# A hybrid attention and delta-rule layer: w_in products taken in another order around the modulations

## Chip, cores and metric

The kernel runs on one core of a Trainium2 chip. The metric is the device time of one execution in microseconds (us), taken as the median of several runs.

## What is computed

One layer for 256 tokens of width 1024 in float32. The part that matters here is the front: a conditioning vector c gives, through silu and a 1024 x 3072 matrix, a shift, a scale and a gate for every channel; x is normalised and modulated to h; h is multiplied by w_in.

```python
mod = silu(c) @ ada_w + ada_b
shift, scale, gate = split(mod, 3)
h = rmsnorm(x, pre_norm_w) * (1 + scale) + shift
proj = h @ w_in            # 1024 x 4104: q, k, v, gates, delta-rule q, k, v, ...
# behind it: softmax attention (8 heads), short convolution and silu on the
# delta-rule q, k, v, the gated delta rule in chunks of 64, output gates
y = concat(o_moba, o_dn) @ w_out
out = x + gate * rmsnorm(y, post_norm_w)
```

## The kernel before

All products are made in split precision: an operand w is kept as whi (rounded) and wlo (w - whi), h as hhi and hlo, and a product is three matmuls into one PSUM tile: whi with hhi, wlo with hhi, whi with hlo (`three`, L1395, L1396, L1397).

Channels of h are cut into 8 blocks k of 128. Of w_in, the 1536 columns of the delta-rule q, k, v come first: 16 units n of 128 x 768, two for each k (k = n // 2). A unit is 6 tiles of 128 columns, so 18 matmuls of 256 columns (`qkv_products`, `qkv_unit_tile`); the last two units are run together, tile pair by tile pair (`last_qkv_products`), and each finished pair is handed on to the convolution. They start when the split parts of both units 14 and 15 are there. Behind them come the other columns of w_in (`half`), and everything else.

Before a unit n can run:
- its weights must have landed (SyncE issues all loads in a hand-written order), ScalarE must have made whi of it (`hi(n)`, L543), and GpSimd (`lo(n)`, L474) or VectorE (`lo(n)`, L915, for n = 5, 9, 11, 14) must have made wlo; `low_part(n)` names that semaphore;
- its block k of h must be there in both parts.

h comes in pieces p = 0 to 5, of blocks 0, 1, 2, 3, (4, 5) and (6, 7). A piece goes through these steps:
- `mod_sums(p, k0, k1)` on VectorE: a sum over the 8 row blocks of the modulation matrix, weighted with silu(c), first one L932, then six L934, then L936 into `acc`; for pieces 4 and 5 these are 128 x 512;
- `mod(p)` on TensorE (L1458): 4 matmuls with one column (8 for pieces 4 and 5) that turn `acc` into columns of shift and scale;
- `modulate(p)` on VectorE (L945, L947): the columns mod_b and mod_a;
- `modulated(p)` on ScalarE (L582): h of each block into a PSUM bank, then `h_hi(p)` (L593): hhi of each block;
- `h_lo(p)` on VectorE (L906): hlo of each block. It waits for hhi of the whole piece.

Every engine runs its own list in the order in which it is written, and waits on semaphores. The lists around the change, as they are before:
- TensorE: ... unit 3, mod(3), units 4, 5, 6, mod(4), units 7, 8, 9, mod(5), units 10 to 13, the last two.
- ScalarE: ... hi(5), piece 2, piece 3, hi(6), hi(7), hi(8), piece 4, hi(9) to hi(13), piece 5, hi(14), the gates' columns, hi(15), hi(16), first taps of the convolution.
- VectorE: ... rest of sums 3, h_lo(2), lo(5), modulate(3), two sums of piece 4, h_lo(3), six sums of piece 4, two sums of piece 5, modulate(4), two more, h_lo(4), lo(9), the last four sums of piece 5, modulate(5), lo(11), h_lo(5), the gates' low part, lo(14), conv.
- GpSimd: lo(0) to lo(4), lo(6), lo(7), lo(8), lo(10), lo(12), lo(13), lo(15), ...

The wait of a unit stands ahead of all its matmuls:

```python
def qkv_products(n):
    k = n // 2
    pe.wait_ge(hlo_done, k + 1)
    pe.wait_ge(*low_part(n))
    for i in range(6 * (n % 2), 6 * (n % 2) + 6):
        ins = qkv_unit_tile(k, i)
    ins.then_inc(unit_done, 1)
```

Of the kernel before, what the change touches and what calls it, by code (L numbers as in the profile page):

```python
# [32 lines left out]
ACT = mybir.ActivationFunctionType  # L33
# [3 lines left out]
P = 128  # L37
D = 1024
S = 256
# [22 lines left out]
PIECES = [(0, 1), (1, 1), (2, 1), (3, 1), (4, 2), (6, 2)]  # L62
# [10 lines left out]
SPL = 4  # L73
# [8 lines left out]
def build(nc, x, x_turned, ada, gate_w, gate_b, post_w, w_qkv, w_rest, w_gates, w_out, const, out):  # L82
    with ExitStack() as ctx:
        def sb(name, shape, dt=F32, into=ctx):
            return into.enter_context(nc.sbuf_tensor(name, shape, dt))
# [4 lines left out]
        bank = [ctx.enter_context(nc.psum_tensor(f"bank{b}", [P, 512], F32)) for b in range(8)]  # L90
# [12 lines left out]
        mod_a = sb("mod_a", [P, NK])  # L103
        mod_b = sb("mod_b", [P, NK])
# [11 lines left out]
        hhi = sb("hhi", [P, NK, S], F32R)  # L116
        hlo = sb("hlo", [P, NK, S], F32R)
        raw = sb("raw", [P, RAW, UNIT])
        whi = sb("whi", [P, SPL, UNIT], F32R)
        wlo = sb("wlo", [P, SPL, UNIT], F32R)  # L120
# [29 lines left out]
        with ExitStack() as e:  # L150
            xT = sb("xT", [P, NK, S], into=e)
# [14 lines left out]
        with ExitStack() as e:  # L166
# [20 lines left out]
        xsq_done, xsq1_done, xrows_ready, xrows_copied, xsum_ready, xstd_done, xrstd_done, rs_ready, xn_done, expa_done = map(  # L187
            sem, ("xsq_done", "xsq1_done", "xrows_ready", "xrows_copied", "xsum_ready", "xstd_done", "xrstd_done", "rs_ready", "xn_done", "expa_done"))
        acc_done, mod_ready, rows_made, rows_copied, mod_read, h_done, hhi_done, hlo_done = map(
            sem, ("acc_done", "mod_ready", "rows_made", "rows_copied", "mod_read", "h_done", "hhi_done", "hlo_done"))  # L190

        hi_done, lo_done, dve_lo_done, unit_done, group_ready = map(sem, ("hi_done", "lo_done", "dve_lo_done", "unit_done", "group_ready"))
# [34 lines left out]
        def raw_u(n):  # L227
            if n < RAW:
                return raw[:, n, 0:HQ]
            if n < N1:  # L230
                return homes[n - RAW]
            return raw[:, (n - N1) % RAW, :]
# [9 lines left out]
        def split_u(buf, n):  # L242
            return buf[:, n % SPL, 0:(HQ if n < N1 else UNIT)]
# [4 lines left out]
        def two(b):  # L248
            return bank[b][:, :].rearrange("p (a s) -> p a s", a=2)
# [66 lines left out]
        def low_part(n):  # L316

            if n in DVE_LO:
                return dve_lo_done, sum(u <= n for u in DVE_LO)
            return lo_done, n + 1 - sum(u <= n for u in DVE_LO)  # L320
# [209 lines left out]
        def _(act):  # L530
# [7 lines left out]
            def hi(n):  # L538

                act.wait_ge(*loaded(n))  # L540
                if n >= SPL:
                    act.wait_ge(*used_up(n - SPL))
                act.activation(split_u(whi, n), raw_u(n), ACT.Copy).then_inc(hi_done, 1)  # L543
# [31 lines left out]
            def modulated(p):  # L575

                k0, n = PIECES[p]
                act.wait_ge(mod_read, p + 1)
                act.wait_ge(xn_done, p + 1)
                for j in range(n):  # L580
                    k = k0 + j
                    act.activation(two(6 + p % 2)[:, j, :], xT[:, k, :], ACT.Identity, scale=mod_a[:, k:k + 1], bias=mod_b[:, k:k + 1]).then_inc(h_done, 1)  # L582

            def h_hi(p):
                k0, n = PIECES[p]
                if p == 0:
                    act.wait_ge(mod_read, 1)
                    act.wait_ge(xn_done, 1)
                    act.activation(hhi[:, 0, :], xT[:, 0, :], ACT.Identity, scale=mod_a[:, 0:1], bias=mod_b[:, 0:1]).then_inc(hhi_done, 1)
                    return  # L590
                act.wait_ge(h_done, k0 + n)
                for k in range(k0, k0 + n):
                    act.activation(hhi[:, k, :], two(6 + p % 2)[:, k - k0, :], ACT.Copy).then_inc(hhi_done, 1)  # L593

            def ba_hi():
                act.wait_ge(wba_loaded, 16)
                act.activation(wbs[:, :, 0:8], wba[:, :, :], ACT.Copy).then_inc(wba_hi, 1)
# [163 lines left out]
            hi(6)  # L761
            hi(7)
            hi(8)
            modulated(4)
            h_hi(4)
            hi(9)
            hi(10)
            hi(11)
            hi(12)
            hi(13)  # L770
            modulated(5)
            h_hi(5)
            hi(14)
            ba_hi()
            hi(15)
            hi(16)
# [83 lines left out]
        def _(dve):  # L860
# [51 lines left out]
            def lo(n):  # L912

                dve.wait_ge(hi_done, n + 1)
                dve.tensor_tensor(split_u(wlo, n), raw_u(n), split_u(whi, n).bitcast(F32), ALU.subtract).then_inc(dve_lo_done, 1)  # L915
# [5 lines left out]
            def mod_sums(p, k0, k1):  # L921

                n = 256 * PIECES[p][1]
                a = bank[6 + p % 2][:, 0:n]
                if k0 == 0:
                    dve.wait_ge(hlo_done, PIECES[p - 1][0])
                for k in range(k0, k1):
                    w, c_k = ada_piece(p)[:, k, :], sml[:, 24 + k:25 + k]
                    if k % 2 == 0:
                        dve.wait_ge(*ada_ready(p, k))  # L930
                    if k == 0:
                        link(dve.tensor_scalar(a, w, c_k, None, ALU.mult))  # L932
                    elif k < NK - 1:
                        link(dve.scalar_tensor_tensor(a, w, c_k, a, ALU.mult, ALU.add))  # L934
                    else:
                        dve.scalar_tensor_tensor(acc[:, p % 2, 0:n], w, c_k, a, ALU.mult, ALU.add).then_inc(acc_done, 1)  # L936

            def modulate(p):

                k0, n = PIECES[p]  # L940
                k2, b = slice(k0, k0 + n), bank[mod_bank(p)]
                dve.wait_ge(mod_ready, p + 1)
                if p == 0:
                    dve.wait_ge(scale_done, 1)
                dve.tensor_tensor(mod_b[:, k2], b[:, 0:n], pcol[:, R_SHIFT + k0:R_SHIFT + k0 + n], ALU.add)  # L945
                for k in range(k0, k0 + n):
                    ins = dve.scalar_tensor_tensor(mod_a[:, k:k + 1], b[:, n + k - k0:n + k - k0 + 1], scale1[:, k:k + 1],  # L947
                                                   pcol[:, R_PRE + k:R_PRE + k + 1], ALU.add, ALU.mult)
                ins.then_inc(mod_read, 1)
# [303 lines left out]
            mod_sums(3, 4, 8)  # L1253
            h_lo(2)
            lo(5)
            modulate(3)
            mod_sums(4, 0, 2)
            h_lo(3)
            mod_sums(4, 2, 4)
            mod_sums(4, 4, 8)  # L1260
            mod_sums(5, 0, 2)
            modulate(4)
            mod_sums(5, 2, 4)
            h_lo(4)
            lo(9)
            mod_sums(5, 4, 8)
            modulate(5)
            lo(11)
            h_lo(5)
# [122 lines left out]
        def _(pe):  # L1392
# [58 lines left out]
            def mod(p):  # L1451

                if p < ROWS:
                    pe.wait_ge(rows_copied, p + 1)
                else:
                    pe.wait_ge(acc_done, p - ROWS + 1)
                for i in range(2 * PIECES[p][1]):
                    ins = pe.matmul(bank[mod_bank(p)][:, i:i + 1], acc[:, p % 2, i * P:(i + 1) * P], epsc[:, 2:3] if p < ROWS else ones[:, 0:1],  # L1458
                                    start=True, stop=True)
                ins.then_inc(mod_ready, 1)  # L1460

            def qkv_unit_tile(k, i):
                n, o = 2 * k + i // 6, (i % 6) * P
                return three(bank[i // 2][:, (i % 2) * S:(i % 2 + 1) * S], w_parts, h_parts,
                             (slice(None), n % SPL, slice(o, o + P)), (slice(None), k, slice(None)),
                             start=(k == 0 and i % 2 == 0), stop=(k == NK - 1), skip=True)
# [6 lines that stand above are left out]
                for i in range(6 * (n % 2), 6 * (n % 2) + 6):  # L1473
                    if k == 0 and i == 10:
                        pe.wait_ge(xn_done, len(PIECES))
                    ins = qkv_unit_tile(k, i)
                ins.then_inc(unit_done, 1)

# [354 lines left out]
            mod(2)  # L1833
            qkv_products(2)
            qkv_products(3)
            mod(3)
            qkv_products(4)
            qkv_products(5)
            qkv_products(6)
            mod(4)  # L1840
            qkv_products(7)
            qkv_products(8)
            qkv_products(9)
            mod(5)
            qkv_products(10)
            qkv_products(11)
            qkv_products(12)
            qkv_products(13)
            last_qkv_products()
            ba()  # L1850
# [168 lines left out]
```

## Time and profile before

| | |
|---|---|
| median of 3 runs | 190.93 us (190.72 to 196.72) |
| the profiled execution, its own time | 190.73 us |
| span of that execution, first to last instruction | 188.9 us |
| around the span (190.73 - 188.9) | 1.8 us |
| TensorE busy | 178.0 us (94%) |
| VectorE busy | 141.5 us (75%) |
| ScalarE busy | 101.5 us (54%) |
| GpSimd busy | 77.5 us (41%) |
| mean granted TensorE clock | 0.996 |
| the 16 units, first to last matmul start | 14.14 to 56.58 us |

How to read it: times are counted from the start of the span. The ends of matmuls are modelled, so a matmul of 256 columns is shown with 0.28 us though the next begins 0.12 us later; it is the starts that tell. An L number is a line of the kernel. Idle time of an engine matters only where the engine is the bound of that stretch.

### The profile page before, as it was taken

Reading aid. Unit: us, or ns where it says so; the run is one execution under the profiler, and the core shown is the slowest. Engines: PE = TensorE matmul, PEld = TensorE weight load, DVE = VectorE, ACT = ScalarE, POOL = GpSimd, SP = SyncE. Lnnn points to the kernel's source line nnn. Section 1 sums busy time; section 2 is a strip of 40 time slices with the busy share of each in tenths; the row PEclk is TensorE's granted clock in tenths of the full one; section 3 lists DMA queues with packets and bytes.
Section 4 is the critical chain, followed back from the end, with each engine's and each line's share of the span. In section 5 each row is a group of like instructions: output and inputs, shape, how many; then the busy total and the mean of one; then the engine's idle time right before and its main releaser. Section 6 shows DMA issues by size and latency. Waiting matters only on the chain.

```text
span 188.9 us, 4380 instructions
## 1 busy us (share of the span) xinstructions
PE 178.0 (94%) x1718; PEld 161.5 (85%) x1718; DVE 141.5 (75%) x345; ACT 101.5 (54%) x195; POOL 77.5 (41%) x42
## 2 busy tenths in 40 slices
PE   7999989889999998999999999999999999999980
PEld 6769879789999998998998999999998987888850
DVE  0359699893459988998999787889689777858074
ACT  2645444439368878956562270455384448636230
POOL 2036627335687922985055068224913200810000
PEclk9999999999999999999999999999999999999998
DMA  5999999999519980300901807006942983020023
GB/s 160 403 386 394 393 409 407 407 397 404 218 16 367 395 328 8 114 0 2 323 14 17 319 8 212 13 0 220 362 201 78 344 356 119 14 97 0 3 111 111
DMA packets 12246, 38.41 MB, mean 203 GB/s; under 512 B 1473, under 2 KB 1857, under 8 KB 11714
## 3 DMA queue, kind: packets, MB, share of 16 engines
q1 hardware_dynamic: 12082, 37.61, 53.6%
q10 hardware_dynamic: 144, 0.52, 0.8%
q8 instruction: 14, 0.23, 0.5%
q14 instruction: 6, 0.05, 0.1%
HBM read 37.08 MB, written 1.05 MB: 202 GB/s over the span
## 4 chain that ended last, share of the span: by engine, by line
PE 69%; DVE 16%; DMA 6%; SPq 5%; issue 2%; ACT 1%; POOL 1%; DVEq 0%; POOLq 0%; ACTq 0%
PE bank L1395 16%; PE bank L1397 15%; PE bank L1396 15%; DVE cv L958 6%; DMA ada<-in_ada 6%; DVE bank L934 4%; SPq L351 3%; PE bank L1641 3%; PE bank L1630 3%; PE bank L1738 2%; PE bank L1745 2%; SPq L368 1%; PE bank L1754 1%; PE bank L1604 1%; PE bank L1666 1%
## 5 line engine op out<-in xcount | busy, mean ns | idle before, releaser
L474 POOL TENSOR_TENSOR wlo<-raw,whi 128x1024 fp32r<-128x1024 f32 (+1 forms) x25 | 58.1, 2334 | 62.2 <-ACT whi L543 62.2
L1395 PE MATMUL bank<-hhi,whi 128*128 128x256 f32 x218 | 63.1, 289 | 1.6 <-DVE hlo L906 1.1
L1396 PE MATMUL bank<-hhi,wlo 128*128 128x256 f32 x218 | 61.6, 283 | 0.0
L1397 PE MATMUL bank<-hlo,whi 128*128 128x256 f32 x218 | 61.6, 283 | 0.0
L1395 PEld LDWEIGHTS bank<-hhi,whi 128*128 128x128 f32 x218 | 41.7, 191 | 3.3 <-issue 1.8
L543 ACT ACTIVATE whi<-raw 128x1024 fp32r<-128x1024 f32 (+1 forms) x33 | 33.3, 1023 | 16.5 <-PE bank L1397 7.4
L1396 PEld LDWEIGHTS bank<-hhi,wlo 128*128 128x128 f32 x218 | 41.8, 192 | 0.0
L1397 PEld LDWEIGHTS bank<-hlo,whi 128*128 128x128 f32 x218 | 41.7, 191 | 0.0
L958 DVE SCALAR_TENSOR_TENSOR cv<-bank,convh,cv 128x255 f32<-128x255 f32 (+2 forms) x36 | 17.0, 481 | 5.6 <-ACT cv L609 4.6
L934 DVE SCALAR_TENSOR_TENSOR bank<-ada,sml,bank 128x256 f32<-128x256 f32 (+1 forms) x24 | 14.9, 621 | 0.7
L1157 DVE SCALAR_TENSOR_TENSOR accg<-ada,sml,accg 128x512 f32<-128x512 f32 x16 | 12.0, 751 | 2.7 <-DMA ada<-in_gate_w 2.3
L1395 PE MATMUL bank<-whi,ohi 128*128 128x512 f32 x32 | 12.6, 393 | 0.0
L1397 PE MATMUL bank<-wlo,ohi 128*128 128x512 f32 x32 | 12.5, 390 | 0.0
L672 ACT ACTIVATE pr<-bank,stat 128x128 f32<-128x128 f32 (+1 forms) x16 | 6.5, 420 | 11.1 <-DVE stat L1122 11.1
L1396 PE MATMUL bank<-whi,olo 128*128 128x512 f32 x32 | 12.4, 389 | 0.0
L915 DVE TENSOR_TENSOR wlo<-raw,whi 128x1024 fp32r<-128x1024 f32 x8 | 9.8, 1222 | 0.8 <-ACT whi L543 0.6
L488 POOL TENSOR_TENSOR rot<-rot,cst 128x512 f32<-128x512 f32 x4 | 4.4, 1092 | 12.5 <-DVE rot L1097 11.8
L1395 PE MATMUL bank<-whi,hhi 128*128 128x256 f32 x32 | 9.2, 286 | 0.0
L1396 PE MATMUL bank<-whi,hlo 128*128 128x256 f32 x32 | 9.1, 283 | 0.0
L1397 PE MATMUL bank<-wlo,hhi 128*128 128x256 f32 x32 | 9.0, 283 | 0.0
L1406 PE MATMUL bank<-ones 128*128 128x256 f32 x22 | 7.9, 530 | 1.1 <-DVE ones L868 1.1
L1406 PEld LDWEIGHTS bank<-ones 128*128 128x128 f32 x22 | 5.9, 279 | 2.3 <-DVE ones L868 1.0
(223 smaller groups left out, 337.6 us busy)
## 6 DMA issues: line engine op xcount, KB each, us to landing
raw<-in_w_rest SPq DMA_DIRECT2D x20, 512.0 KB, 4.8
ada<-in_ada SPq DMA_DIRECT2D x16, 256.0 KB, 7.1
ada<-in_ada SPq DMA_DIRECT2D x8, 512.0 KB, 12.0
ada<-in_gate_w SPq DMA_DIRECT2D x4, 1024.0 KB, 6.9
raw<-in_w_out SPq DMA_DIRECT2D x8, 512.0 KB, 5.7
raw<-in_w_qkv SPq DMA_DIRECT2D x5, 384.0 KB, 8.2
qkvs<-in_w_qkv SPq DMA_DIRECT2D x4, 384.0 KB, 11.2
cv<-in_w_qkv SPq DMA_DIRECT2D x4, 384.0 KB, 12.7
```

The lines of the kernel that those rows point to most:

```text
L351: sp.dma_start(ada_piece(p)[:, 2 * g:2 * g + 2, :].rearrange("p k n -> p (k n)"), ada[:, o:o + n * 512]).then_inc(ada_ready(p, 2 * g)[0], 16)
L474: pool.tensor_tensor(split_u(wlo, n), raw_u(n), split_u(whi, n).bitcast(F32), ALU.subtract).then_inc(lo_done, 1)
L543: act.activation(split_u(whi, n), raw_u(n), ACT.Copy).then_inc(hi_done, 1)
L672: act.activation(pr[:, e, o:o + w], bank[ATT[e]][:, o:o + w], ACT.Exp, scale=AD ** -0.5, bias=stat[:, 16 + i:17 + i], accum_out=stat[:, 32 ...
L915: dve.tensor_tensor(split_u(wlo, n), raw_u(n), split_u(whi, n).bitcast(F32), ALU.subtract).then_inc(dve_lo_done, 1)
L934: link(dve.scalar_tensor_tensor(a, w, c_k, a, ALU.mult, ALU.add))
L958: ins = dve.scalar_tensor_tensor(cv[:, i, j:], b[:, 0:S - j], w, cv[:, i, j:], ALU.mult, ALU.add)
L1157: dve.scalar_tensor_tensor(a, adag[:, k, :], sml[:, 24 + k:25 + k], a, ALU.mult, ALU.add).then_inc(gate_acc, 1)
L1395: pe.matmul(out, a[0][ia], b[0][ib], start=start, stop=False, skip_group_check=skip)
L1396: pe.matmul(out, a[1][ia], b[0][ib], start=False, stop=False, skip_group_check=skip)
L1397: return pe.matmul(out, a[0][ia], b[1][ib], start=False, stop=stop, skip_group_check=skip)
L1406: pe.matmul(bank[b][:, 0:256], ones[:, :], ones[:, 0:1].to_broadcast([P, 256]), start=True, stop=True)
```

## The change

On TensorE, units 4, 6, 8 and 12 take the six tiles' products with hhi first (12 matmuls) and the six with hlo last, and wait for hlo only ahead of those (`qkv_h_lo_last`). Units 9, 10 and 11 take the products with whi first and those with wlo last, and wait for wlo only there (`qkv_w_lo_last`). mod(3) stands behind unit 4 instead of ahead of it, mod(4) amid unit 7 after four of its six tiles (`qkv_around_mod`) instead of ahead of it, mod(5) behind unit 10 instead of ahead of it. On ScalarE pieces 4 and 5 go block by block (`h_two`). On VectorE two sums of piece 4 stand ahead of modulate(3) instead of behind it, and one sum of piece 5 is moved from ahead of modulate(4) to behind it. The number of matmuls is the same.

```diff
+            def h_two(p):
+                k0, n = PIECES[p]
+                act.wait_ge(mod_read, p + 1)
+                act.wait_ge(xn_done, p + 1)
+                for k in range(k0, k0 + n):
+                    act.activation(two(6 + p % 2)[:, k - k0, :], xT[:, k, :], ACT.Identity, scale=mod_a[:, k:k + 1], bias=mod_b[:, k:k + 1]).then_inc(h_done, 1)
+                    act.wait_ge(h_done, k + 1)
+                    act.activation(hhi[:, k, :], two(6 + p % 2)[:, k - k0, :], ACT.Copy).then_inc(hhi_done, 1)
...
-            modulated(4)
-            h_hi(4)
+            h_two(4)
...
-            modulated(5)
-            h_hi(5)
+            h_two(5)
...
+            mod_sums(4, 0, 2)
             modulate(3)
-            mod_sums(4, 0, 2)
+            mod_sums(4, 2, 3)
             h_lo(3)
-            mod_sums(4, 2, 4)
-            mod_sums(4, 4, 8)
-            mod_sums(5, 0, 2)
+            mod_sums(4, 3, 8)
+            mod_sums(5, 0, 1)
             modulate(4)
-            mod_sums(5, 2, 4)
+            mod_sums(5, 1, 3)
             h_lo(4)
             lo(9)
-            mod_sums(5, 4, 8)
+            mod_sums(5, 3, 8)
             modulate(5)
...
+            def qkv_first_parts(n, second, n0=0, n1=6):
+
+                k = n // 2
+                for i in range(6 * (n % 2) + n0, 6 * (n % 2) + n1):
+                    o = (i % 6) * P
+                    out = bank[i // 2][:, (i % 2) * S:(i % 2 + 1) * S]
+                    w, h = whi[:, n % SPL, o:o + P], hhi[:, k, :]
+                    pe.matmul(out, w, h, start=False, stop=False, skip_group_check=True)
+                    if second == "w_lo":
+                        pe.matmul(out, wlo[:, n % SPL, o:o + P], h, start=False, stop=False, skip_group_check=True)
+                    else:
+                        pe.matmul(out, w, hlo[:, k, :], start=False, stop=False, skip_group_check=True)
+
+            def qkv_h_lo_last(n):
+
+                k = n // 2
+                pe.wait_ge(hhi_done, k + 1)
+                pe.wait_ge(*low_part(n))
+                qkv_first_parts(n, "w_lo")
+                pe.wait_ge(hlo_done, k + 1)
...
+            def qkv_w_lo_last(n):
+
+                k = n // 2
+                pe.wait_ge(hlo_done, k + 1)
+                pe.wait_ge(hi_done, n + 1)
+                qkv_first_parts(n, "h_lo")
+                pe.wait_ge(*low_part(n))
...
+            def qkv_around_mod(n, p):
+
+                k = n // 2
+                pe.wait_ge(hlo_done, k + 1)
+                pe.wait_ge(*low_part(n))
+                for i in range(6 * (n % 2), 6 * (n % 2) + 6):
+                    if i % 6 == 4:
+                        mod(p)
+                    ins = qkv_unit_tile(k, i)
+                ins.then_inc(unit_done, 1)
...
+            qkv_h_lo_last(4)
             mod(3)
-            qkv_products(4)
             qkv_products(5)
-            qkv_products(6)
-            mod(4)
-            qkv_products(7)
-            qkv_products(8)
-            qkv_products(9)
+            qkv_h_lo_last(6)
+            qkv_around_mod(7, 4)
+            qkv_h_lo_last(8)
+            qkv_w_lo_last(9)
+            qkv_w_lo_last(10)
             mod(5)
-            qkv_products(10)
-            qkv_products(11)
-            qkv_products(12)
+            qkv_w_lo_last(11)
+            qkv_h_lo_last(12)
             qkv_products(13)
             last_qkv_products()
```

## Rows read from the trace of the kernel before

**Rows 1.** The page's first part: busy time of each engine.

```profile
PE 178.0 (94%) x1718; PEld 161.5 (85%) x1718; DVE 141.5 (75%) x345; ACT 101.5 (54%) x195; POOL 77.5 (41%) x42
```

**Rows 2.** Who waited for whom, 15 to 70 us: us in total, times, longest.

```profile
PE bank L1458 <- DVE acc L936: 1.7, 3, 0.8
...
PE bank L1395 <- DVE hlo L906: 1.1, 1, 1.1
...
PEld bank L1395 <- issue: 0.8, 2, 0.4
```

**Rows 3.** Timeline of TensorE, 17 to 53 us: start, us, what, idle before.

```profile
17.27 0.35 PE L1395 MATMUL bank<-hhi,whi 128*128 128x256 f32 x1 [0.38 <-POOL wlo L474]
...
26.15 0.61 PE L1458 MATMUL bank<-ones,acc 128*128 128x1 f32 x4 [0.83 <-DVE acc L936]
26.61 0.36 PE L1395 MATMUL bank<-hhi,whi 128*128 128x256 f32 x1
...
31.31 0.36 PE L1395 MATMUL bank<-hhi,whi 128*128 128x256 f32 x1
...
34.06 1.05 PE L1458 MATMUL bank<-ones,acc 128*128 128x1 f32 x8 [0.36 <-DVE acc L936]
...
38.44 0.39 PE L1395 MATMUL bank<-hhi,whi 128*128 128x256 f32 x1 [1.06 <-DVE hlo L906]
...
42.85 0.95 PE L1458 MATMUL bank<-ones,acc 128*128 128x1 f32 x8
43.66 0.36 PE L1395 MATMUL bank<-hhi,whi 128*128 128x256 f32 x1
...
52.38 0.28 PE L1395 MATMUL bank<-hhi,whi 128*128 128x256 f32 x1
```

**Rows 4.** Timeline of VectorE, 27 to 45 us.

```profile
27.21 0.15 DVE L945 TENSOR_TENSOR mod_b<-bank,cst 128x1 f32<-128x1 f32 x1
27.28 0.21 DVE L947 SCALAR_TENSOR_TENSOR mod_a<-bank,scale,cst 128x1 f32<-128x1 f32 x1
27.40 0.75 DVE L932 TENSOR_SCALAR bank<-ada,sml 128x512 f32<-128x512 f32 x1
...
29.31 3.91 DVE L934 SCALAR_TENSOR_TENSOR bank<-ada,sml,bank 128x512 f32<-128x512 f32 x5
...
37.96 0.76 DVE L906 TENSOR_TENSOR hlo<-bank,hhi 128x256 fp32r<-128x256 f32 x2 [0.43 <-ACT hhi L593]
...
43.84 0.16 DVE L945 TENSOR_TENSOR mod_b<-bank,cst 128x2 f32<-128x2 f32 x1 [1.23 <-PE bank L1458]
...
44.16 0.95 DVE L915 TENSOR_TENSOR wlo<-rot,whi 128x768 fp32r<-128x768 f32 x1
```

**Rows 5.** Timeline of ScalarE, 24 to 50 us.

```profile
24.77 0.38 ACT L593 ACTIVATE hhi<-bank 128x256 fp32r<-128x256 f32 x1
27.52 0.57 ACT L582 ACTIVATE bank<-xT,mod_b,mod_a 128x256 f32<-128x256 f32 x1 [2.37 <-DVE mod_a L947]
28.12 0.39 ACT L593 ACTIVATE hhi<-bank 128x256 fp32r<-128x256 f32 x1
28.40 0.84 ACT L543 ACTIVATE whi<-early 128x768 fp32r<-128x768 f32 x1
...
48.77 0.84 ACT L543 ACTIVATE whi<-cv 128x768 fp32r<-128x768 f32 x1 [1.12 <-DMA cv<-in_w_qkv]
```

**Rows 6.** Timeline of GpSimd, 15 to 50 us.

```profile
15.29 1.83 POOL L474 TENSOR_TENSOR wlo<-raw,whi 128x768 fp32r<-128x768 f32 x1 [1.64 <-ACT whi L543]
...
29.31 1.85 POOL L474 TENSOR_TENSOR wlo<-early,whi 128x768 fp32r<-128x768 f32 x1 [4.72 <-ACT whi L543]
...
49.69 1.84 POOL L474 TENSOR_TENSOR wlo<-cv,whi 128x768 fp32r<-128x768 f32 x1 [1.06 <-ACT whi L543]
```

**Rows 7.** Stretches: busy us of PE, PEld, DVE, ACT, POOL, then TensorE's granted clock.

```profile
37.20:38.50 1.30, 0.23 (x3) 0.06 (x1) 0.87 (x3) 1.30 (x4) 0.00 (x0) 1.00 1.01 392
...
187.00:188.00 1.00, 0.00 (x0) 0.00 (x0) 0.00 (x0) 0.00 (x0) 0.00 (x0) 0.72 0.93 342
```

More of the change, by code:

```diff
@@ L1475, in qkv_products @@
                         pe.wait_ge(xn_done, len(PIECES))
+                    ins = qkv_unit_tile(k, i)
[18 more added lines that the diff above has]
+                for i in range(6 * (n % 2), 6 * (n % 2) + 6):
+                    o = (i % 6) * P
+                    ins = pe.matmul(bank[i // 2][:, (i % 2) * S:(i % 2 + 1) * S], whi[:, n % SPL, o:o + P], hlo[:, k, :],
+                                    start=False, stop=False, skip_group_check=True)
+                ins.then_inc(unit_done, 1)
+            def qkv_w_lo_last(n):
[4 more added lines that the diff above has]
+                pe.wait_ge(*low_part(n))
+                for i in range(6 * (n % 2), 6 * (n % 2) + 6):
+                    o = (i % 6) * P
+                    ins = pe.matmul(bank[i // 2][:, (i % 2) * S:(i % 2 + 1) * S], wlo[:, n % SPL, o:o + P], hhi[:, k, :],
+                                    start=False, stop=False, skip_group_check=True)
+                ins.then_inc(unit_done, 1)
+            def qkv_around_mod(n, p):
+                k = n // 2
+                pe.wait_ge(hlo_done, k + 1)
+                pe.wait_ge(*low_part(n))
+                for i in range(6 * (n % 2), 6 * (n % 2) + 6):
+                    if i % 6 == 4:
+                        mod(p)
                     ins = qkv_unit_tile(k, i)
```

## The prediction

> **What bounds the kernel now.** I read the busy shares first: TensorE is at work for 94% of the span [rows 1], so what counts is when it stands still, and the change touches only the stretch of the 16 units. Then who waited for whom there [rows 2]: TensorE waited 1.7 us for sums of VectorE ahead of mod(), 1.1 us for hlo, and its weight load is shown with 0.8 us of "issue", a wait with no releaser named. Third, TensorE's timeline [rows 3], which turns this into places. A unit without a stop takes 18 x 0.12 = 2.16 us, and the first matmul behind a stop costs 0.08 us more: units 10 to 13 run from 43.66 to 52.38, 8.72 us = 4 x 2.16 + 0.08. mod() with 4 matmuls takes 0.46 us (26.15 to 26.61), with 8 it takes 0.81 us (42.85 to 43.66). The stops, counted from the slot that was free (0.16 us ahead of a modelled end):
> - ahead of mod(3): 25.16 to 26.15, 0.99 us;
> - ahead of unit 6: 26.61 + 0.08 + 2 x 2.16 = 31.01, start 31.31, 0.30 us;
> - ahead of mod(4): 31.31 + 0.08 + 2.16 = 33.55, start 34.06, 0.51 us;
> - ahead of unit 8: 34.06 + 0.81 + 0.08 + 2.16 = 37.11, start 38.44, 1.33 us by this count.
>
> Together 3.1 us, and mod(5) and all behind it up to 52.38 run without a stop. The last pair of units starts at 52.38; VectorE's convolution and the rest of TensorE's list hang on that start, so I take it as the time that the change moves.
>
> **Behind the stops: the chain of the weights.** Unit 6 is the one to look at, since the waits view names nobody for it. GpSimd's lo(6) runs 29.31 + 1.85 = 31.16 [rows 6] and unit 6 starts at 31.31, 0.15 us later. At unit 1, where the profile does name GpSimd, lo(1) ends at 15.29 + 1.83 = 17.12 and the matmul starts at 17.27: the same 0.15 us [rows 3, 6]. So lo(6) released unit 6. lo(6) began 0.07 us behind hi(6) on ScalarE (28.40 + 0.84 = 29.24), and hi(6) came directly behind the two steps of piece 3 (27.52, 28.12), which began 0.03 us after VectorE's modulate(3) was done (27.28 + 0.21 = 27.49) [rows 4, 5]. So modulate(3) holds not only piece 3 of h but also unit 6's weights: from its end to the start of unit 6 it is 31.31 - 27.49 = 3.82 us.
>
> **The change part by part, in TensorE's new order.**
>
> Unit 4 ahead of mod(3). It needs hhi of block 2, done at 24.77 + 0.38 = 25.15 [rows 5], so it starts at about 25.2, runs 12 matmuls to 26.7, and hlo of block 2 is made by 26.5 (0.42 us directly behind the sum that released mod(3) at 26.15): no second stop. It ends at 25.2 + 0.08 + 2.16 = 27.44. The 0.99 us are gone. mod(3) costs 0.46: 27.90.
>
> modulate(3) later. Two sums of 512 columns now stand ahead of it on VectorE. A sum takes 3.91 / 5 = 0.78 us, 0.79 with its step [rows 4]. They begin at 27.21 where modulate(3) began, if the data have landed (they had by 27.40, [rows 4], so at most 0.19 us is open), and mod_a is done at 27.49 + 2 x 0.79 = 29.07 instead of 27.49. mod(3) itself, done near 28.05, doesn't hold it. ScalarE then does piece 3 from 29.10, hhi(3) at 30.09, and hi(6) from 29.98 to 30.82.
>
> Unit 6. lo(6) on GpSimd: 30.89 to 32.74. Unit 5 ends at 27.90 + 0.08 + 2.16 = 30.14. Unit 6 takes its hhi products first, but those include wlo with hhi, so its first wait is for lo(6) too: start 32.74 + 0.15 = 32.89. A stop of 2.75 us where there were 0.30, and unit 6 is 1.58 us later than before (32.89 against 31.31), exactly the two sums. Everything won at mod(3) waits here. hlo(3) is made at about 30.5, long before its turn: that late wait is worth nothing in this unit.
>
> Unit 7 around mod(4). Unit 6 ends at 32.89 + 2.24 = 35.13; lo(7) follows lo(6), 32.74 + 1.85 = 34.59, in time. Sums 4: one from 28.99, then h_lo(3) near 30.1 to 30.47, then five, 30.47 + 5 x 0.79 = 34.4. mod(4) comes after four tiles, 35.13 + 1.44 = 36.57, so its 0.51 us stop is gone. It is read by VectorE 0.99 us after its start, as mod(5) was (42.85 to 43.84), at 37.56; ScalarE is released 0.44 us later, 38.0. The two tiles left run 36.57 + 0.81 + 0.08 + 0.72 = 38.18.
>
> Unit 8. With h_two the first hhi is there 0.99 us after ScalarE's start (27.52 to 28.12 + 0.39, [rows 5]), 38.99; unit 8 starts at 39.1, a stop of 0.9 us in place of 1.33, 0.65 us later than before. The second block follows 0.9 us later (the next instruction begins 0.28 us behind L593), so hhi(5) is at 39.9 and h_lo(4), which waits for both, makes hlo(4) by 40.4 (0.42 us each in the pair, [rows 4]); the six hlo products are due at 39.1 + 0.08 + 1.44 = 40.6. No stop. Without h_two and the late wait the start would be at about 40.5: these two edits are worth 1.4 us here.
>
> Units 9 and 10. hi(9) 39.8 to 40.6, lo(9) on VectorE 40.7 to 41.6, due at 42.8; hi(10) to 41.4, lo(10) on GpSimd to 43.3, due at 44.9. Both covered by the late wait for wlo. 41.34 + 2 x 2.16 = 45.66.
>
> mod(5). The last five sums of piece 5 begin behind lo(9): 41.53 + 5 x 0.79 = 45.5, just ahead of 45.66, no stop. mod(5) to 46.47. modulate(5) starts at 46.65, lo(11) 0.32 us behind it [rows 4] ends at 46.97 + 0.95 = 47.92; unit 11 wants it at 46.47 + 0.08 + 1.44 = 47.99. Covered by 0.07 us; if it misses, the price is the miss plus 0.15.
>
> Units 11 to 13. h_two(5) starts at 47.1, hhi(6) 48.1 ahead of unit 12 at 48.71; hlo(6) at 49.45, due 50.15. Last start: 46.47 + 0.08 + 3 x 2.16 = 53.03. hi(14), the gates' columns and hi(15) on ScalarE end near 50.8, lo(14) on VectorE near 51.8 and lo(15) on GpSimd at 52.65: in time, 0.4 us of cover.
>
> The sum: 53.03 - 52.38 = +0.65 us. Check by stops: taken away 0.99 + 0.30 + 0.51 + 1.33 = 3.13; put in 0.04 (unit 4) + 2.75 + 0.92 = 3.71, difference 0.58, the rest is rounding in the modelled mod(4). Regrouped matmuls cost nothing: the same 18 loads and 18 products in a unit, each step still 0.12 us; no row shows a wait inside a unit that is already met; bounds by the nearest row, the 0.08 us of a restart, are one lost or one won at each of the seven new waits, so -0.56 to +0.56, and I take 0, since the waits at unit starts that are already met show none. SyncE's queue isn't moved: the sums of piece 3, for which load of piece 5 waits, end as before. Behind 53.03 the convolution and all after it shift with the start. Against the profiled execution: 190.73 + 0.65 = 191.4; the median lies 0.2 above it, so I forecast 191.5.
>
> **Rivals.**
> (a) Unit 6 isn't held by GpSimd, as the view's "issue" would have it [rows 2]. Then units 4 to 6 run from 25.2 to 32.4, mod(4) waits for the sums (34.4) inside unit 7, and the last start would be near 50.95. But another limit stands there: hi(15) waited for its DMA until 48.77 [rows 5], lo(15) ran 49.69 + 1.84 = 51.53 [rows 6], plus 0.15 = 51.68. So the gain ends at 52.38 - 51.68 = 0.70 us, 190.2. For it: the name in the view. Against it: the 0.15 us that fits twice, and lo(6)'s place in the list. The same time is the floor for any way in which the stops vanish.
> (b) The clock falls in the new stop ahead of unit 6, the longest in this stretch. The granted clock stayed at 1.00 (2.4 GHz) over the present stop at 37.2 to 38.5; it is 0.72 in 187 to 188, falling towards 1.2 GHz, 4 us after TensorE's last matmul [rows 7]. A stop of 2.75 us lies between. If it falls, unit 6 runs at half speed from 32.89: 18 x 0.12 = 2.16 us more (an estimate from the full-speed step), and with mod(4), units 7 and 8 behind it, the end is 0.65 + 2.16 = 2.8 us late, 193.7; two units of it, 195.9. It decides from the point where the stop is long enough for the gate. The Trainium skill ("TensorE: Matmul & The Clock Gate", "Why this matters for your kernels") warns of just this: an idle gap between bursts of matmuls can send the clock back to half. By that rule this change is slower than its ledger; the trace has a fall only behind a longer silence, so it gets a small chance.
> (c) The thin covers (lo(11) 0.07, mod(5) 0.15, lo(15) 0.4 us) fail together: at most some 0.8 us more, 192.3.
>
> **How the numbers follow.** Forecast 0.65, rival (a) 0.22, (b) 0.06, (c) 0.07. The range of 189.8 to 192.6 holds the forecast with the 0.56 us of the new waits either way, (a) with 0.4 us to spare, and (c); (b) is left out. Faster by over 2% means below 187.1, slower means above 194.7; 2% is about what a measurement of this kernel tells from no change. Only the two-unit form of (b) reaches beyond on the slow side, and on the fast side rival (a)'s floor speaks against it: 0.02 faster, 0.95 within, 0.03 slower.
>
> **What would show it.** Right: in the new trace L945 of piece 3 starts near 28.8, hi(6) near 30.0, lo(6) near 30.9, and unit 6 stands until 32.9; no stop ahead of mod(3), mod(4), mod(5); a stop of 0.9 us ahead of unit 8; the last pair of units starting near 53.0 instead of 52.38. Wrong: unit 6 starts by 31 while lo(6) still runs (then (a)), the granted clock is under 1.00 behind 32.9 (then (b)), or the last pair starts where I say and the end doesn't follow, because something behind the convolution waits for its data.

## The result, and the profile after

The changed kernel takes 193.19 us (median; 193.04 to 193.75 in four runs) against 191.36 us, or 190.93 us without an execution of 196.72; the ratio without that one is 1.0119, with a 95% interval of 1.0099 to 1.0138. It is 2.3 us slower, where 0.65 us slower was forecast, and outside the range of 189.8 to 192.6. The profiled execution took 193.75 us with a span of 191.8 us and a mean granted clock of 0.988 (before: 190.73, 188.9 and 0.996). Some executions of every kernel, that of 196.72 among them, take 4 to 8 us longer at a lower mean clock; no ratio or time below counts them, and where such a one was profiled (the filled stop, and before with the sums ahead) its clock is 1.00 up to 145 us, behind every row shown from it.

First TensorE's timeline of the kernel after, around units 4 to 8 (start, us, what, idle before; L1465 is mod(), L1493 and L1495 the products with hhi of the regrouped units, L1508 their products with hlo, L1402 to L1404 the old form):

```profile
25.49 0.38 PE L1493 MATMUL bank<-hhi,whi 128*128 128x256 f32 x1
...
27.74 0.50 PE L1465 MATMUL bank<-ones,acc 128*128 128x1 f32 x4
28.10 0.36 PE L1402 MATMUL bank<-hhi,whi 128*128 128x256 f32 x1
...
33.14 0.36 PE L1493 MATMUL bank<-hhi,whi 128*128 128x256 f32 x1 [2.65 <-POOL wlo L474]
...
34.30 0.41 PE L1495 MATMUL bank<-hhi,wlo 128*128 128x256 f32 x1
34.51 0.41 PE L1493 MATMUL bank<-hhi,whi 128*128 128x256 f32 x1
34.73 0.41 PE L1495 MATMUL bank<-hhi,wlo 128*128 128x256 f32 x1
...
36.65 0.41 PE L1402 MATMUL bank<-hhi,whi 128*128 128x256 f32 x1
...
38.29 0.95 PE L1465 MATMUL bank<-ones,acc 128*128 128x1 f32 x8
...
40.83 0.39 PE L1493 MATMUL bank<-hhi,whi 128*128 128x256 f32 x1 [0.77 <-ACT hhi L602]
```

The stops ahead of mod(3) and mod(4) [rows 3] are gone. In their place stands one of 2.65 us ahead of unit 6 (2.80 from slot to slot), and now the profile names GpSimd as its releaser. From 33.7 us on the matmuls behind it start 0.21 us apart instead of 0.12. The stretches of the same profile say why (busy PE, PEld, DVE, ACT, POOL, then the granted clock):

```profile
32.00:33.00 1.00, 0.00 (x0) 0.00 (x0) 0.96 (x2) 0.00 (x0) 1.00 (x2) 1.00 1.02 390
33.00:34.00 1.00, 0.86 (x6) 0.89 (x7) 0.93 (x3) 0.85 (x1) 1.00 (x1) 0.86 1.01 400
34.00:35.00 1.00, 1.00 (x7) 1.00 (x6) 1.00 (x2) 0.00 (x0) 1.00 (x2) 0.50 1.02 399
...
36.00:37.00 1.00, 1.00 (x6) 1.00 (x6) 0.00 (x0) 0.00 (x0) 0.57 (x1) 0.50 1.06 414
37.00:38.00 1.00, 1.00 (x10) 1.00 (x9) 0.00 (x0) 0.00 (x0) 0.00 (x0) 0.93 0.96 380
```

The granted clock goes to 1.2 GHz (0.50) at about 33.7 us, half a microsecond after unit 6 started and not while TensorE stood, and is back at 2.4 GHz at 37.1. Unit 6 takes 36.65 - 33.14 = 3.51 us instead of 2.24, and the four tiles of unit 7 take 1.64 instead of 1.44: 1.47 us in all.

The chain that makes the stop, on VectorE (first fence), ScalarE (second) and GpSimd (third) of the kernel after:

```profile
27.50 0.75 DVE L939 TENSOR_SCALAR bank<-ada,sml 128x512 f32<-128x512 f32 x1
28.28 0.76 DVE L941 SCALAR_TENSOR_TENSOR bank<-ada,sml,bank 128x512 f32<-128x512 f32 x1
29.07 0.16 DVE L952 TENSOR_TENSOR mod_b<-bank,cst 128x1 f32<-128x1 f32 x1
```

```profile
29.40 0.57 ACT L582 ACTIVATE bank<-xT,mod_b,mod_a 128x256 f32<-128x256 f32 x1 [3.96 <-DVE mod_a L954]
30.00 0.39 ACT L593 ACTIVATE hhi<-bank 128x256 fp32r<-128x256 f32 x1
30.28 0.84 ACT L543 ACTIVATE whi<-early 128x768 fp32r<-128x768 f32 x1
```

```profile
31.19 1.81 POOL L474 TENSOR_TENSOR wlo<-early,whi 128x768 fp32r<-128x768 f32 x1 [6.30 <-ACT whi L543]
...
45.06 3.64 POOL L474 TENSOR_TENSOR wlo<-cv,whi 128x768 fp32r<-128x768 f32 x2
```

Against [rows 4 to 6]: modulate(3) starts at 29.07 instead of 27.21, hi(6) at 30.28 instead of 28.40, lo(6) at 31.19 instead of 29.31: 1.9 us each, of which 0.29 us is an offset that this trace has before any of the edits can act (the first sum of piece 3 starts at 22.04 instead of 21.75). The forecast had 28.8, 30.0 and 30.9 without that offset. The last pair of units starts at 54.86 instead of 52.38, and the convolution 2.48 us later (56.65 against 54.17). The span grew by 2.9 us: some 0.4 us more came behind that start, and no run tells from what.

### The profile page after: what moved, and what is told of

Same layout as the page of the kernel before. It is cut to its first block, busy times and chain, and to the rows that moved or that the text cites. A ratio compares the mean times of both kernels' runs of the same rounds, so it can differ in the third digit from the quotient of the medians.

```text
span 191.8 us, 4383 instructions
## 1 busy us (share of the span) xinstructions
PE 179.8 (94%) x1718; PEld 163.1 (85%) x1718; DVE 140.6 (73%) x345; ACT 101.6 (53%) x195; POOL 77.4 (40%) x42
## 3 DMA queue, kind: packets, MB, share of 16 engines
HBM read 37.08 MB, written 1.05 MB: 199 GB/s over the span
## 4 chain that ended last, share of the span: by engine, by line
PE 69%; DVE 13%; DMA 5%; SPq 5%; issue 2%; ACT 2%; POOL 2%; DVEq 0%; ACTq 0%; POOLq 0%
PE bank L1402 13%; PE bank L1403 13%; PE bank L1404 13%; DVE cv L965 6%; DMA ada<-in_ada 5%; SPq L351 3%; PE bank L1698 3%; PE bank L1687 3%; PE bank L1493 3%; DVE bank L941 2%; PE bank L1795 2%; PE bank L1802 2%; PE bank L1508 1%; SPq L368 1%; PE bank L1495 1%
## 5 line engine op out<-in xcount | busy, mean ns | idle before, releaser
L1402 PE MATMUL bank<-hhi,whi 128*128 128x256 f32 x176 | 51.1, 290 | 0.4 <-POOL wlo L474 0.4
L1403 PE MATMUL bank<-hhi,wlo 128*128 128x256 f32 x176 | 49.9, 283 | 0.0
L1404 PE MATMUL bank<-hlo,whi 128*128 128x256 f32 x176 | 49.7, 283 | 0.0
L1402 PEld LDWEIGHTS bank<-hhi,whi 128*128 128x128 f32 x176 | 33.8, 192 | 1.8 <-issue 1.7
L1403 PEld LDWEIGHTS bank<-hhi,wlo 128*128 128x128 f32 x176 | 33.8, 192 | 0.0
L1404 PEld LDWEIGHTS bank<-hlo,whi 128*128 128x128 f32 x176 | 33.8, 192 | 0.0
L1493 PE MATMUL bank<-hhi,whi 128*128 128x256 f32 x42 | 11.3, 303 | 3.4 <-POOL wlo L474 2.6
L1402 PE MATMUL bank<-whi,ohi 128*128 128x512 f32 x32 | 12.6, 392 | 0.0
L1404 PE MATMUL bank<-wlo,ohi 128*128 128x512 f32 x32 | 12.5, 390 | 0.0
L1493 PEld LDWEIGHTS bank<-hhi,whi 128*128 128x128 f32 x42 | 8.4, 200 | 3.9 <-issue 2.8
L1402 PE MATMUL bank<-whi,hhi 128*128 128x256 f32 x32 | 9.2, 286 | 0.0
L1404 PE MATMUL bank<-wlo,hhi 128*128 128x256 f32 x32 | 9.0, 283 | 0.0
```

The costliest lines, as they stand in the source:

```text
L1402: pe.matmul(out, a[0][ia], b[0][ib], start=start, stop=False, skip_group_check=skip)
L1403: pe.matmul(out, a[1][ia], b[0][ib], start=False, stop=False, skip_group_check=skip)
L1404: return pe.matmul(out, a[0][ia], b[1][ib], start=False, stop=stop, skip_group_check=skip)
L1493: pe.matmul(out, w, h, start=False, stop=False, skip_group_check=True)
```

## The experiments

Each ratio is against the kernel before, run on the same chip in turns; its runs took 190.6 to 191.9 us. "Over before" is the ratio turned into us. "Clock" is the mean granted clock of a run; the kernel before had 0.991 to 0.999 in its runs.

**Filling the stop.** TensorE gets something to do ahead of unit 6 that is short enough not to hold unit 6 up: 20 matmuls whose weights, the tile `zero`, are all 0, so that the sums stay as they are. The lines that make `zero` are left out here.

```diff
+            def fill(n):
+                pe.wait_ge(zero_set, 1)
+                for _ in range(n):
+                    pe.matmul(bank[0][:, 0:S], zero[:, :], hhi[:, 0, :], start=False, stop=False, skip_group_check=True)
...
             qkv_products(5)
+            fill(20)
             qkv_h_lo_last(6)
```

> The kernel after, with TensorE's stop ahead of unit 6 filled by 20 matmuls with an all-zero stationary tile, added to the sums (they add 0; 20 x 0.12 = 2.4 us, less than the 2.9 us from slot to slot of the stop, so unit 6 still starts when lo(6) releases it). Theory (the stop itself costs 0.6 us over before, and the clock that falls behind it costs the other 1.5 us): granted clock 1.00 from 30 to 40 us, unit 6 starts at the same time as after (about 33.1), the last pair of units 1.5 us earlier than after; time 0.7 us over before, about 191.9. Rival (the clock is no part of it, the regrouped matmuls or the waits between them cost the 2 us): the time stays that of after, 2 us over before. Rival (the clock falls whatever TensorE does there): clock 0.5 near 34 us as after, and 2 us over before.

Measured: ratio 1.0084 (1.0059 to 1.0110), so 1.6 us over before, and a clock of 0.993 to 0.998. TensorE's timeline of this kernel:

```profile
30.05 2.56 PE L1546 MATMUL bank<-hhi,zero 128*128 128x256 f32 x20
32.87 0.36 PE L1499 MATMUL bank<-hhi,whi 128*128 128x256 f32 x1 [0.27 <-POOL wlo L478]
...
36.54 0.95 PE L1471 MATMUL bank<-ones,acc 128*128 128x1 f32 x8
...
48.97 0.98 PE L1527 MATMUL bank<-hhi,wlo 128*128 128x256 f32 x6 [0.84 <-DVE wlo L928]
```

The clock stays at 1.00, and from unit 6 to mod(4) it is 36.54 - 32.87 = 3.67 us, where the kernel after needs 38.29 - 33.14 = 5.15: the 1.5 us are back at this place. So it is behind the empty stop that the clock falls, and with the stop filled it didn't, by the mean clock of all nine counted executions of the two filled kernels (0.993 to 0.998); and the regrouped matmuls cost nothing (unit 4 of the kernel after takes 27.74 - 25.49 = 2.25 us, where 2.24 were reckoned). But the total got only some 0.7 us of it, and by the totals alone even that is not clear of noise (the kernel after had 1.0099 to 1.0138): a new stop of 0.84 us stands amid unit 11, where the kernel after has none. VectorE and GpSimd of the filled kernel there, then VectorE of the kernel after:

```profile
46.97 1.95 DVE L928 TENSOR_TENSOR wlo<-rot,whi 128x768 fp32r<-128x768 f32 x1
```

```profile
44.46 3.64 POOL L478 TENSOR_TENSOR wlo<-cv,whi 128x768 fp32r<-128x768 f32 x2 [1.12 <-ACT whi L547]
```

```profile
48.73 0.95 DVE L922 TENSOR_TENSOR wlo<-rot,whi 128x768 fp32r<-128x768 f32 x1
```

lo(11) on VectorE takes 1.95 us instead of 0.95 [rows 4]. It ends at 48.92, 0.82 us behind the end of GpSimd's lo(12) and lo(13) at 48.10, as if it had stood until GpSimd was done; two runs below test that. In the kernel after lo(11) began at 48.73, GpSimd's pair ended at 45.06 + 3.64 = 48.70, and it took 0.95 us. The fall of the clock had moved it out of the way, by 0.03 us.

**The sums behind modulate(3) again.** The rest is the kernel after.

```diff
-            mod_sums(4, 0, 2)
             modulate(3)
-            mod_sums(4, 2, 3)
+            mod_sums(4, 0, 2)
             h_lo(3)
+            mod_sums(4, 2, 3)
```

> The kernel after, with the two sums of piece 4 put back behind modulate(3) on VectorE. Theory: modulate(3) is then released by mod(3) at about 28.3 instead of 29.1, hi(6) and lo(6) come 0.8 us earlier, the stop ahead of unit 6 is about 2.0 us in place of 2.9, the granted clock stays at 1.00; the time is that of before within 0.4 us. Rival (clock no part): only the 0.8 us come back, 1.4 us over before. Rival (2.0 us of standing still already drops the clock): 1.3 us over before, with a clock of 0.5 behind unit 6's start.

Measured: ratio 1.0037 (0.9998 to 1.0077), but the mean hides two kinds of run. Seven took 191.0 to 191.7 us at a mean clock of 0.991 to 0.998, three took 193.0 to 193.5 at 0.987 or 0.988. The profiled one is of the second kind:

```profile
32.24 0.36 PE L1493 MATMUL bank<-hhi,whi 128*128 128x256 f32 x1 [1.85 <-POOL wlo L474]
```

```profile
33.00:34.00 1.00, 1.00 (x7) 1.00 (x6) 0.96 (x2) 0.75 (x1) 1.00 (x2) 0.52 1.02 401
```

The stop is 0.80 us shorter, as expected, and yet the clock fell in this execution (0.52, where a mean of 1.00 was expected): by time and mean clock the theory and its second rival are both right, in different executions of one kernel, though only the kind with the fall was profiled. A fall costs this kernel 2.0 us (193.2 against 191.2, means of the two kinds), not the 1.3 of the rival. Some 0.3 us of it stand amid unit 11 in the profile, where lo(11), begun at 47.83 beside GpSimd's lo(13), takes 1.40 us. Without a fall, and with the two sums back in their place, the change costs no time that can be told from noise.

**hi(6) ahead of piece 3 on ScalarE.**

```diff
+            hi(6)
             modulated(3)
             h_hi(3)
-            hi(6)
```

> The kernel after, with hi(6) ahead of piece 3 on ScalarE, where ScalarE waits 4 us. Theory: lo(6) is done before 30.3, unit 6 starts as soon as unit 5 and hhi of block 3 are there (about 30.5), no clock fall; a short stop (0.3 to 0.5 us) for lo(7) ahead of unit 7; the gain is then capped by lo(15), whose weights come by DMA, at 0.7 us under before, so 0.3 to 0.8 us faster than before. Rival (something else than the weights holds unit 6): the stop stays, 2 us over before.

Measured: ratio 0.9994 (0.9963 to 1.0025). Eight of nine runs took 190.7 to 191.3 us, 0.2 us under before; one took 193.19 at a mean clock of 0.983, and why isn't known. The stop ahead of unit 6 is gone (it starts at 30.22), the one ahead of unit 7 is 0.34 us, as expected; but most of the gain isn't there. It is spent in the same place as in the filled kernel (TensorE, then VectorE):

```profile
32.97 0.36 PE L1402 MATMUL bank<-hhi,whi 128*128 128x256 f32 x1 [0.34 <-POOL wlo L474]
...
47.23 0.98 PE L1521 MATMUL bank<-hhi,wlo 128*128 128x256 f32 x6 [0.96 <-DVE wlo L922]
```

```profile
45.10 2.07 DVE L922 TENSOR_TENSOR wlo<-rot,whi 128x768 fp32r<-128x768 f32 x1
```

**The kernel before with the sums ahead of modulate(3), nothing else.**

```diff
-            modulate(3)
             mod_sums(4, 0, 2)
+            modulate(3)
```

> The kernel before, with one edit alone: the two sums of piece 4 ahead of modulate(3). TensorE's order is that of before, with mod(3) ahead of unit 4. Theory: hi(6) and lo(6) 1.58 us later, unit 6 starts at 32.9, a stop of 1.9 us in place of 0.3; the stop ahead of mod(4) is 0.1 to 0.5 us, unit 8 is about 1.15 us late, the clock stays at 1.00 because the stop is 1.9 us and not 2.9; 1.1 us over before. Rival (a stop of 1.9 us drops the clock too): 2.5 us over before, granted clock 0.5 near 34 us. Rival (the sums are not what delays unit 6): same time as before.

Measured: ratio 1.0086 (1.0056 to 1.0115), 1.6 us over before, at a clock of 0.992 to 0.994. The two sums alone, in TensorE's old order, make the kernel slower, with no fall of the clock:

```profile
32.92 0.36 PE L1395 MATMUL bank<-hhi,whi 128*128 128x256 f32 x1 [1.68 <-POOL wlo L474]
...
39.49 0.39 PE L1395 MATMUL bank<-hhi,whi 128*128 128x256 f32 x1 [0.91 <-DVE hlo L906]
...
47.72 0.36 PE L1395 MATMUL bank<-hhi,whi 128*128 128x256 f32 x1 [0.60 <-DVE wlo L915]
```

Unit 6 starts at 32.9, as expected, and unit 8 1.05 us late, where 1.15 was. The 0.5 us beyond the forecast are the third row: unit 11 waits for lo(11), which took 2.34 us here, from 45.23 on, beside GpSimd's lo(12).

**lo(11) ahead of modulate(5), with hi(6) first.** This tests the meeting of the two engines; it is the kernel of the hi(6) run with one more edit.

```diff
+            lo(11)
             modulate(5)
-            lo(11)
```

> The kernel after with hi(6) ahead of piece 3 (as in the run with that edit alone, which measured no difference from before), and lo(11) on VectorE ahead of modulate(5) instead of behind it. Theory (VectorE's subtraction lo(11) cannot run while GpSimd's lo(12) or lo(13) runs, which cost 0.96 us ahead of unit 11's last products): lo(11) runs at about 43.7, as soon as hi(11) is done and before lo(12) begins, in 0.95 us; the stop of 0.96 us amid unit 11 is gone; the last pair of units is then held by lo(15), near 51.7; 0.7 us faster than before. Rival (the stop amid unit 11 came from the load of its weights): hi(11) stays at 42.9, so the stop stays, same time as before.

Measured: ratio 0.9968 (0.9956 to 0.9981), 190.14 to 190.89 in six runs, 0.6 us faster than before, where 0.7 was expected. VectorE, and the only stop of TensorE between the start of unit 8 and the end of the units:

```profile
44.03 0.96 DVE L922 TENSOR_TENSOR wlo<-rot,whi 128x768 fp32r<-128x768 f32 x1 [0.31 <-ACT whi L543]
```

```profile
51.97 0.36 PE L1402 MATMUL bank<-hhi,whi 128*128 128x256 f32 x1 [0.53 <-POOL wlo L474]
```

lo(11) takes 0.96 us. It is not quite done (44.99) when GpSimd's lo(12) begins at 44.80, but it came first, and the price falls on GpSimd: its pair takes 3.71 us instead of 3.64. The stop amid unit 11 is gone. What holds the last pair of units now is lo(15), the cap of rival (a). This version beats both kernels, the one before by 0.3%.

**lo(11) ahead of modulate(5), in the filled kernel.** The same edit there.

> The kernel with the filled stop, and lo(11) ahead of modulate(5). Theory: the 0.84 us stop amid unit 11, which the filled kernel has and the kernel after does not, comes from the meeting of lo(11) with GpSimd's lo(13); ahead of modulate(5) lo(11) meets lo(12) only and is done by 47.2, before unit 11 wants it; 0.8 us less than the filled kernel, so 0.8 us over before, which is what the stop ahead of unit 6 alone costs. Rival (the filled kernel is slow for another reason): 1.6 us over before, as the filled kernel.

Measured: ratio 1.0036 (1.0019 to 1.0052), 0.7 us over before. lo(11) met lo(12) alone (45.34 to 47.12), and the 0.84 us are back. What is left is close to what the ledger of the prediction gave for the stop without a fall of the clock, 0.65 us; the last pair of units starts at 53.20, 0.2 us of it waiting for lo(15), which the prediction had given 0.4 us of cover.

**The same edit in the kernel after.**

> The kernel after with lo(11) ahead of modulate(5), no other edit. In the kernel after lo(11) begins 0.03 us behind the end of GpSimd's lo(13) and takes 0.95 us. Theory: moved ahead it starts at 47.1 amid lo(12) and lo(13), takes until one of them ends, at the latest 49.5, and modulate(5) and piece 5 of h are up to 1.1 us late; unit 12 waits for hhi; 0.3 to 0.6 us slower than after, 2.6 us over before. Rival (the two engines do not hold each other up): lo(11) 0.95 us, same time as after.

Measured: ratio 1.0123 (1.0077 to 1.0169). The mean again covers two kinds. Two executions took 193.94 and 194.33 us at a mean clock of 0.990 and 0.986, 2.9 us over before, where the kernel after is 2.3 over: that is the way I expected (2.6), but on two executions. The third, 192.09 us at 0.998, is the profiled one, and the most telling of the study, because in it the clock did not fall:

```profile
33.35 0.36 PE L1493 MATMUL bank<-hhi,whi 128*128 128x256 f32 x1 [2.63 <-POOL wlo L474]
```

```profile
34.00:35.00 1.00, 1.00 (x11) 1.00 (x10) 0.96 (x3) 0.09 (x1) 1.00 (x2) 1.00 1.03 401
```

A stop of 2.63 us with a clock of 1.00 behind it, and a time 0.9 us over before. My expectation for lo(11) had taken the fallen clock's timetable for granted: without the fall it met lo(12) alone and lasted 1.80 us, within its cover.

**The load of unit 15 earlier**, on top of the best version.

```diff
             load_unit(14)
+            load_unit(15)
             load_unit(19)
             load_unit(17)
             load_gates()
             load_unit(18)
-            load_unit(15)
```

> The same as the kernel with hi(6) and lo(11) first, and the load of unit 15 issued directly behind that of unit 14 instead of behind those of four others. Theory (the DMA of unit 15 and lo(15) cap the gain): hi(15) no longer waits for a DMA, the last pair of units starts near 51.4, 0.9 to 1.0 us faster than before. Rival (another limit right behind it, such as lo(14) or unit 16's weights for the first half): 0.7 us faster, as without the new load order.

Measured: ratio 0.9997 (0.9972 to 1.0023). Of twelve runs five took 190.0 to 190.4 us at 0.993 to 0.996, the other seven 191.0 to 192.1 at 0.987 to 0.992. In the profiled one (190.13) hi(15) no longer waits and the stop at the last pair is gone, but TensorE then waits longer ahead of the gates' matmuls, 1.44 us instead of 0.82. A second set of runs was to show where the clock falls in the slower executions (its text counts six and six where the runs are five and seven):

> The kernel with unit 15's load early, unchanged: of its 12 runs 6 took 190.0 to 190.4 us at a mean clock of 0.993 to 0.996, and 6 took 191.0 to 192.1 us at 0.987 to 0.992. Theory: the slower ones hold a clock fall of about 3 us at half speed, in or behind the 1.4 us stop near 71 us ahead of the gates' matmuls, which is longer than in before (0.8 us). Rival: it lies at the stops of the units (30 to 40 us). The profile shows the place if its run is one of the slower kind.

Measured: ratio 1.0004 (0.9976 to 1.0032), again two kinds (190.3 to 190.95 at 0.993 to 0.997, 191.3 to 191.9 at 0.986 to 0.989). The profiled one was of the first kind, with a stop of 1.86 us at 71.51 and a clock of 1.00 on both sides of it. Where the clock falls in the others is open. On the mean the early load of unit 15 gains nothing over the best version (1.0004 and 0.9997 against 0.9968): its quicker kind, 190.2 us in the first set, is 0.3 us under the best version's mean of 190.5, and its slower kind takes the gain away.

**The kernel after again.**

> The kernel after, unchanged, to see how its time goes with the granted clock of each run. Theory (the clock falls behind the stop of 2.8 us ahead of unit 6 in most runs, not in all; where it doesn't, lo(11) meets GpSimd's lo(13) as in the filled kernel and costs 0.84 us): runs with a mean clock over 0.991 take 1.5 to 1.7 us more than before, runs under 0.989 take 2.1 to 2.4 us more; most are of the second kind. Rival (the fall costs its whole 1.5 us): runs over 0.991 take 0.6 to 0.8 us more than before.

Measured: ratio 1.0122 (1.0096 to 1.0148). Four runs at 0.989 or 0.990 took 193.02 to 193.95, 2.3 us over the 191.2 of before; one at 0.993 took 192.90, 1.7 over. The profiled one shows 0.50 from 34 to 37 us. It fits the theory, but the kind without a fall is one run.

**Piece 4 and unit 8 as before**, on the best version.

```diff
-            h_two(4)
+            modulated(4)
+            h_hi(4)
...
-            qkv_h_lo_last(8)
+            qkv_products(8)
```

> The kernel with hi(6) and lo(11) first, with piece 4 of h and unit 8 as in the kernel before (both blocks modulated, then both hhi, and unit 8 waiting for hlo ahead of its first matmul). Theory (the split is worth about 1.4 us at unit 8, of which 0.5 us was spent standing ahead of the last pair of units anyway): the stop ahead of unit 8 is 2.3 us instead of 0.9, the 0.5 us stop ahead of the last pair is gone, 0.9 us slower than the kernel with both edits, 0.2 us over before; a clock fall in some runs is possible. Rival (the late wait is worth nothing): same time as the kernel with both edits.

Measured: ratio 1.0103 (1.0070 to 1.0136), 2.5 us slower than with the split instead of 0.9. The longer stop is as expected, the total isn't:

```profile
38.45 0.39 PE L1403 MATMUL bank<-hhi,whi 128*128 128x256 f32 x1 [2.06 <-DVE hlo L914]
```

```profile
40.00:54.00 14.00, 14.00 (x108) 14.00 (x106) 6.50 (x13) 6.90 (x11) 7.46 (x5) 0.88 0.72 283
```

The stop ahead of unit 8 is 2.06 us instead of 0.77, 1.3 us longer (the prediction gave the split 1.4 us), and behind it the clock falls: a mean of 0.88 over 14 us is 3.4 us at half speed (0.12 x 14 / 0.5). All four runs were at 0.981 to 0.990.

## Why the prediction was wrong

The step that failed is rival (b): the fall of the clock behind the new stop got a chance of 0.06, no term in the sum and no room in the range. It came in nearly every execution and took 1.47 us at units 6 and 7. With the forecast's 0.65 us for the stop that makes 2.1 of the 2.3 us measured. A second step failed unseen beneath it, the cover of lo(11). The rest of the ledger held.

- Unit 4 ahead of mod(3), the sums ahead of modulate(3), hi(6), lo(6), the stop ahead of unit 6: all came as worked out, within 0.1 us once the 0.29 us offset of this trace is taken off (unit 6: 32.89 forecast, 33.14 - 0.29 = 32.85). That lo(6) released unit 6, read from a match of 0.15 us, was right; rival (a) is out.
- mod(4) without a stop, 0.9 us ahead of unit 8, units 9, 10 and 11 covered by the late wait, lo(11) covered by 0.07 us: all as forecast, the last of them by luck, as told below. With the 1.47 us of the clock and the offset added, unit 8 was due at 40.86 (it started at 40.83) and the last pair at 54.79 (54.86).
- Where the clock stays up and lo(11) is out of the way (the filled kernel with lo(11) first), the time is 0.7 us over before, beside the forecast of 0.65. The one profiled execution of the unfilled stop without a fall (lo(11) first) is 0.9 us over.
- The clock. I set a stop of 2.75 us between one of 1.3 us without a fall and a silence of 4 us with one, and gave the fall 0.06. It came in both profiles of the kernel after, by the mean clock in eight of its nine runs, and in two of three of the kernel with lo(11) first, which has the same stop. The Trainium skill ("TensorE: Matmul & The Clock Gate", "Why this matters for your kernels") advises against idle gaps between bursts of matmuls, though its figure is for gaps somewhat longer than this one. The traces go further than the page: the clock fell behind 2.65 and 2.64 us in the kernel after and behind 1.85 us in the run with the sums behind modulate(3). And the profiled execution of the kernel with lo(11) first (2.63 us, clock 1.00) shows that such a gap need not do it. The price of a fall, too, was taken from a wrong step: a matmul is 0.21 us apart at 1.2 GHz, not 0.24, so 1.5 us and not 2.2.
- A term was missing, and the fall hid it. The fall costs 1.5 us where it happens, but by the totals only about 0.7 us (ratio 1.0119 and 1.0122 against 1.0084 of the filled kernel; the intervals overlap), because without it lo(11) runs into GpSimd's lo(12) and lo(13) and TensorE stands 0.84 us longer. So it is 0.65 for the stop and then either 0.84 for the meeting or 1.5 for the fall, not both. That lo(11) kept its 0.07 us in the kernel after is luck: the fall had moved it past GpSimd's pair. With the clock up the forecast of 0.65 would have been too low by some 0.9 us, if the filled kernel (1.6 us over) may stand for it: the covered lo(11) was "covered by 0.07 us; if it misses, the price is the miss plus 0.15", and the miss is 0.8 us. The trace of before had a sign of it: GpSimd's lo(12) and lo(13), begun while VectorE's lo(11) was at work, are shown there as

```profile
44.48 4.16 POOL L474 TENSOR_TENSOR wlo<-cv,whi 128x768 fp32r<-128x768 f32 x2 [3.19 <-ACT whi L543]
```

  4.16 us for the two, where the kernel after has 3.64.
- The change does do what it says at the places that it names. It removed 1.8 us of stops (0.99 at mod(3), 0.51 at mod(4), 0.3 at unit 8) and put 2.5 more ahead of unit 6: 1.6 of them because VectorE's two sums went ahead of the step on which the next weights hang, the rest because TensorE, early from mod(3), waits for the same weights. (The 1.33 us that the prediction counts ahead of unit 8 before the change are 1.22: mod(4) took 0.92 us there, not 0.81.) The two sums alone, in the old order, cost 1.6 us; with them back behind modulate(3) and no fall, the change costs nothing.

## What to carry to other kernels

Before work is moved ahead of a small step, follow everything that is queued behind that step on the engine it feeds: here modulate(3) fed piece 3 of h, but ScalarE's list had the next unit's weights behind it. One long stop of TensorE can be dearer than several short ones of the same sum, because behind it the clock may be down; a time that comes in two kinds with two mean clocks is a sign of it, and the mean of such runs says little about the edit. A thin cover (0.07 us) is to be priced by what happens when it misses, with what the other engines do at that moment, and elementwise work that VectorE and GpSimd both do on operands in SBUF is to be kept apart in time.

## What the runs showed of the hardware

- The granted clock fell to 1.2 GHz 0.6 to 1.5 us behind the start of the matmuls that follow a stop, not in the stop, and was back some 3.4 us later (four profiles with a fall). It fell after stops of 2.65 and 2.64 us in the two profiles of the kernel after, of 2.06 us in the run with unit 8 as before and of 1.85 us in the one with the sums behind; it stayed up after one of 2.63 us (lo(11) first), one of 1.86 us (unit 15's load early) and one of 1.68 us (before with the sums ahead). The length of the stop alone doesn't decide it; what else does wasn't tried.
- At 1.2 GHz a 128x128 by 256 product with its weight load goes on every 0.21 us, at 2.4 GHz every 0.12 us, so a fall costs a factor of 1.8 here and not of 2.
- A VectorE subtraction of two SBUF operands does not go on while a GpSimd one that began first is running: lo(11) takes 0.95 us alone, and 1.40, 1.78, 1.80, 1.95, 2.07 and 2.34 us in the six profiles where it began during lo(12) or lo(13). In all six it ended 0.82 to 0.85 us behind the end of the GpSimd instruction that it met (an estimate where that was lo(12), whose end is taken at half of an undisturbed pair, 1.82 us). The other way round too: where lo(12) or lo(13) began while lo(11) was still due or at work, GpSimd's pair took up to 4.37 us instead of 3.64. VectorE's sums with one operand in PSUM (L934, 0.78 us each) show no such stretch beside GpSimd's lo(6) and lo(7) [rows 4, 6]. The Trainium skill ("GPSIMD Engine Reference", "Specifications") says that the SBUF interfaces are shared with VectorE, with contention for instructions with two SBUF inputs; the trace agrees, with 1.95 us for 0.95 in the filled kernel.
